# Forget gate and index key in one product, the meta tokens' square sums moved, and the spatial bias added by VectorE

## The reference

```
h = rms_norm(x, norm_g)
(a_u, a_v, a_z, b_q, b_c, b_qi, b_ki, b_wi, b_z, c_b, c_c, c_x, c_z,
 d_q, d_k, d_v, d_f, d_z, gates) = split(h @ w_in)

# branch a: spatial gating
v = layer_norm(a_v, ln_g, ln_b)                       # in chunks of 128 tokens, 4 groups of 128
mixed = einsum('gts,bcsge->bctge', tril(w_s), v) + b_s[token, group]
y_a = a_u * mixed * silu(a_z)

# branch b: a sparse attention; k_idx = b_ki (64 columns) picks each query's keys
score = sum_h b_wi[h] * relu(b_qi[h] . b_ki)          # the best 64 keys of each query are kept

# branch d: forgetting attention; d_f has 4 columns, one for each head
cum = cumsum(log_sigmoid(d_f + b_f))
logits = q . k / sqrt(128) + cum[query] - cum[key]

# second layer, ahead of its first product
hn = rms_norm(concat([meta_tokens, x']), norm1_g)
```

## Time and profile before

| | |
|---|---|
| median of three runs | 1201.8 us |
| span of the profiled execution | 1201.2 us |
| its time beyond the median | -0.6 us |
| PE busy | 1056.9 us (88%) |
| DVE busy | 491.7 us (41%) |
| ACT busy | 356.6 us (30%) |
| POOL busy | 387.8 us (32%) |
| chain that ended last, by engine | PE 60%, DMA 27%, DVE 8% |

### The profile page before, as it was taken

One profiled execution on the slowest core, in us unless ns is written; L12 is line 12 of the kernel. 1 busy time (PEld: TensorE's weight loads), 2 busy tenths in 40 slices (PEclk: granted clock), 3 DMA queues, 4 the chain that ended last, 5 costly groups with the idle time before them and its releaser, 6 DMA issues.

```text
span 1201.2 us, 20207 instructions
## 1 busy us (share of the span) xinstructions
PE 1056.9 (88%) x8237; PEld 852.8 (71%) x8237; DVE 491.7 (41%) x973; ACT 356.6 (30%) x536; POOL 387.8 (32%) x176
## 2 busy tenths in 40 slices
PE   9999999999999999999999998977676676767776
PEld 7999999999999999798989787443333333333334
DVE  4447944701125886667854413221111111111113
ACT  4544253444447557234252103100000000000002
POOL 4867568887877766133030000000000000000000
PEclk8999899999999998999999999998888888888898
DMA  6645446466656444113221685999999999999994
GB/s 232 197 127 157 121 143 201 148 185 185 191 167 205 154 143 140 53 54 140 80 91 43 276 332 213 417 428 428 428 428 428 428 428 429 428 428 428 428 413 178
DMA packets 41552, 303.95 MB, mean 253 GB/s; under 512 B 4869, under 2 KB 5253, under 8 KB 27786
## 3 DMA queue, kind: packets, MB, share of 16 engines
q1 hardware_dynamic: 41194, 302.43, 66.4%
q10 hardware_dynamic: 288, 0.52, 0.1%
HBM read 301.89 MB, written 1.05 MB: 252 GB/s over the span
## 4 chain that ended last, share of the span: by engine, by line
PE 60%; DMA 27%; DVE 8%; issue 1%; ACT 1%; SPq 1%; POOL 1%; DVEq 0%; ACTq 0%; POOLq 0%
DMA arena<-down 20%; PE bank L447 11%; PE bank L448 11%; PE bank L449 11%; PE bank L818 9%; PE bank L1273 4%; DMA weights<-gate_up 4%; PE bank L1256 3%; DMA arena<-gate_up 3%; PE bank L782 1%; DVE arena L1948 1%; PE bank L1227 1%; PE bank L1285 1%; PE bank L1018 1%; PE bank L997 1%
## 5 line engine op out<-in xcount | busy, mean ns | idle before, releaser
L2733 POOL TENSOR_TENSOR rounded<-weights,rounded 128x1024 fp32r<-128x1024 f32 x152 | 368.6, 2452 | 175.7 <-ACT rounded L1350 164.0
L447 PE MATMUL bank<-rounded 128*128 128x256 f32 (+2 forms) x784 | 223.0, 284 | 0.7 <-POOL rounded L2733 0.7
L449 PE MATMUL bank<-rounded 128*128 128x256 f32 (+2 forms) x784 | 221.7, 283 | 0.0
L448 PE MATMUL bank<-rounded 128*128 128x256 f32 (+2 forms) x784 | 221.5, 282 | 0.0
L1350 ACT ACTIVATE rounded<-weights 128x1024 fp32r<-128x1024 f32 x146 | 147.1, 1052 | 85.0 <-PE bank L449 56.0
L447 PEld LDWEIGHTS bank<-rounded 128*128 128x128 f32 (+1 forms) x784 | 147.8, 189 | 2.9 <-POOL rounded L2733 1.2
L448 PEld LDWEIGHTS bank<-rounded 128*128 128x128 f32 (+1 forms) x784 | 147.1, 188 | 0.6 <-issue 0.5
L449 PEld LDWEIGHTS bank<-rounded 128*128 128x128 f32 (+1 forms) x784 | 146.7, 187 | 0.2
L447 PE MATMUL bank<-rounded,rounded 128*128 128x256 f32 (+3 forms) x456 | 131.8, 289 | 2.1 <-DVEq L2178 0.8
L448 PE MATMUL bank<-rounded,rounded 128*128 128x256 f32 (+3 forms) x456 | 130.4, 286 | 0.0
L449 PE MATMUL bank<-rounded,rounded 128*128 128x256 f32 (+3 forms) x456 | 130.2, 286 | 0.0
(11 more groups left out here) (444 smaller groups left out, 1348.5 us busy)
## 6 DMA issues: line engine op xcount, KB each, us to landing
weights<-front SPq DMA_DIRECT2D x152, 512.0 KB, 4.3
arena<-down SPq DMA_DIRECT2D x30, 2048.0 KB, 20.6
weights<-gate_up SPq DMA_DIRECT2D x28, 2048.0 KB, 33.4
arena<-gate_up SPq DMA_DIRECT2D x28, 2048.0 KB, 33.2
weights<-front SPq DMA_DIRECT2D x8, 2048.0 KB, 8.3
arena<-gate_up SPq DMA_DIRECT2D x4, 1536.0 KB, 32.9
weights<-gate_up SPq DMA_DIRECT2D x4, 1024.0 KB, 15.3
arena<-down SPq DMA_DIRECT2D x4, 1024.0 KB, 8.0
```

The source lines that it names most:

```text
L447: nc.tensor.matmul(out, a[0], b[1], start=start, stop=False)
L448: nc.tensor.matmul(out, a[0], b[0], start=False, stop=False)
L449: return nc.tensor.matmul(out, a[1], b[0], start=False, stop=stop)
L2733: nc.gpsimd.tensor_tensor(lo, raw[q % RAW], hi.bitcast(f32), ALU.subtract).then_inc(sem("w_lo"), 1)
```

## The change

1. The columns of the weight block are laid out anew, with the index key's 64 ahead of the forget gate's 4, and both are one product of 68 columns. The forget values then lie on partitions 64 to 67 (the slice `F`), and so do `sel` and `b_f`.
2. The square sums of the meta tokens leave the start and get a fill of their own, `meta_rows` in bank 4, behind the first group. What DVE and ACT make of them is moved behind the scaled `c` and the index key.
3. `b_s` is loaded to all 128 partitions, the eight matmuls that added it (one row of ones by `b_s`) are gone, and DVE adds it to the two banks in place ahead of the products of branch a.

```diff
@@ tensor engine
             f = begin("rms_rows", (2,))
-            pe.wait_ge(sem("squares"), 5)
-            for k in range(KD):
-                nc.tensor.matmul(f.bank[:, SEQ:SEQ + META], ones, meta_sq[:, k, :], start=k == 0, stop=k == KD - 1)
             pe.wait_ge(sem("rstd"), 1)
             token_rows(f, rstd1)
             warm_up(banks[5], 2)
...
-            ff_, fk, fc = begin("f", WK, 0), begin("ki", PJ, 0), begin("c", WK, 0)
-            last = {}
+            fk = begin("ki", PJ, 0)
+            turn[WK] += 1
+            fc = begin("c", WK, 0)
...
                 matmul3(fc.bank[:, 0:P + 4], rows_of(k, 0, P), part(w, at, P + 4), first, stop)
-                last["f"] = matmul3(ff_.bank[0:NH, 0:SEQ], part(w, at + 132, NH), rows_of(k), first, stop)
-                last["ki"] = matmul3(fk.bank[0:IDX, 0:SEQ], part(w, at + 136, IDX), rows_of(k), first, stop)
-            end(ff_, last["f"])
-            end(fk, last["ki"])
+                last = matmul3(fk.bank[0:IDX + NH, 0:SEQ], part(w, at + 132, IDX + NH), rows_of(k), first, stop)
+            end(fk, last)
...
             end(fc, last)
+            f = begin("meta_rows", (4,))
+            pe.wait_ge(sem("squares"), 5)
+            for k in range(KD):
+                last = nc.tensor.matmul(f.bank[:, 0:META], ones, meta_sq[:, k, :], start=k == 0, stop=k == KD - 1)
+            end(f, last)
...
-                        nc.tensor.matmul(o, av[:, t, gr * P:(gr + 1) * P], wsT[:, gr, :], start=True, stop=False)
-                        last = nc.tensor.matmul(o, ones[0:1, :], bs[0:1, gr * P:(gr + 1) * P], start=False, stop=True)
+                        last = nc.tensor.matmul(o, av[:, t, gr * P:(gr + 1) * P], wsT[:, gr, :], start=True, stop=True)
@@ scalar engine
-            act.wait_ge(sem("variance"), 2)
-            nc.scalar.activation(meta_var, meta_var, ACT.Sqrt).then_inc(sem("deviation"), 1)
             quarter_hi(5)
...
-            f = got("f")
+            f = got("ki")
...
+            act.wait_ge(sem("variance"), 2)
+            nc.scalar.activation(css, css, ACT.Sqrt).then_inc(sem("deviation"), 1)
             act.wait_ge(sem("variance"), 3)
-            nc.scalar.activation(css, css, ACT.Sqrt).then_inc(sem("deviation"), 1)
+            nc.scalar.activation(meta_var, meta_var, ACT.Sqrt).then_inc(sem("deviation"), 1)
@@ vector engine, behind the copy of the index key
+            meta_bank = got("meta_rows")
+            link(nc.vector.tensor_scalar(meta_var, meta_bank.bank[:, 0:META], 1.0 / D, EPS, ALU.mult, ALU.add))
+            dve.sem_inc(sem("variance"), 1)
...
+            dve.wait_ge(sem("deviation"), 3)
+            meta_row = meta_bank.bank[:, META:2 * META]
+            link(nc.vector.reciprocal(meta_row, meta_var))
+            for k in range(KD):
+                last = nc.vector.scalar_tensor_tensor(meta_n[:, k, :], res[:, k, 0:META], col("norm1_g", k), meta_row,
+                                                      ALU.mult, ALU.mult)
@@ vector engine, behind top_scores(1)
+            for i in range(2):
+                f = got(f"mx{i}")
+                mixed = f.bank[:, :].rearrange("p (j t s) -> p j t s", j=2, t=TT)
+                b_s = bs[:, 2 * i * P:(2 * i + 2) * P].rearrange("p (j s) -> p j s", j=2).unsqueeze(2).to_broadcast([P, 2, TT, P])
+                link(nc.vector.tensor_tensor(mixed, mixed, b_s, ALU.add))
             for i in range(2):
                 times(f"mx{i}", i, y[0][:, 2 * i:2 * i + 2, :], "az", "y0", cpad[:, 2 * i:2 * i + 2, 0:SEQ])
```

More of the change, by code:

```diff
@@ L421, in build @@
         FRONT = A["front"]
+        F = slice(IDX, IDX + NH)
         def two(bank):
@@ L606, in _ @@
                 for j in range(2):
-                    last = nc.tensor.matmul(f.bank[:, j * SEQ:(j + 1) * SEQ], sel[0:NH, 2 * i + j, 0:P], ff[0:NH, 4, :],
+                    last = nc.tensor.matmul(f.bank[:, j * SEQ:(j + 1) * SEQ], sel[F, 2 * i + j, 0:P], ff[F, 4, :],
                                             start=True, stop=True)
@@ L1412, in _ @@
             last.then_inc(sem("css"), 1)
-            f = got("f")
+            f = got("ki")
             act.wait_ge(sem("cols_in"), 16)
-            link(nc.scalar.activation(ff[0:NH, 0, :], f.bank[0:NH, 0:SEQ], ACT.Identity, bias=col("b_f")[0:NH]))
-            act.sem_inc(free[f.b], 1)
+            link(nc.scalar.activation(ff[F, 0, :], f.bank[F, 0:SEQ], ACT.Identity, bias=col("b_f")[F]))
+            act.sem_inc(sem("css"), 1)
+            act.wait_ge(sem("variance"), 2)
+            nc.scalar.activation(css, css, ACT.Sqrt).then_inc(sem("deviation"), 1)
             act.wait_ge(sem("variance"), 3)
-            nc.scalar.activation(css, css, ACT.Sqrt).then_inc(sem("deviation"), 1)
+            nc.scalar.activation(meta_var, meta_var, ACT.Sqrt).then_inc(sem("deviation"), 1)
             evacuate("qi", qi, "qiki")
-            link(nc.scalar.activation(ff[0:NH, 1, :], ff[0:NH, 0, :], ACT.Abs))
-            link(nc.scalar.activation(ff[0:NH, 1, :], ff[0:NH, 1, :], ACT.Exp, scale=-1.0))
-            nc.scalar.activation(ff[0:NH, 1, :], ff[0:NH, 1, :], ACT.Ln, bias=1.0).then_inc(sem("ln_f"), 1)
+            link(nc.scalar.activation(ff[F, 1, :], ff[F, 0, :], ACT.Abs))
+            link(nc.scalar.activation(ff[F, 1, :], ff[F, 1, :], ACT.Exp, scale=-1.0))
+            nc.scalar.activation(ff[F, 1, :], ff[F, 1, :], ACT.Ln, bias=1.0).then_inc(sem("ln_f"), 1)
             evacuate("dq0", dq[:, 0:2, :], "dq", scale=P ** -0.5)
@@ L1888, in _ @@
             dve.sem_inc(free[sums.b], 1)
-            nc.vector.tensor_scalar(meta_var, row_bank.bank[:, SEQ:SEQ + META], 1.0 / D, EPS, ALU.mult,
-                                    ALU.add).then_inc(sem("variance"), 1)
+            dve.sem_inc(free[row_bank.b], 1)
             link(nc.vector.tensor_tensor(both_g, cols[:, COLS["final_g"][0]:COLS["final_g"][1]],
                                          cols[:, COLS["norm1_g"][0]:COLS["norm1_g"][1]], ALU.mult))
-            dve.wait_ge(sem("deviation"), 2)
-            meta_row = row_bank.bank[:, SEQ + META:SEQ + 2 * META]
-            link(nc.vector.reciprocal(meta_row, meta_var))
-            for k in range(KD):
-                last = nc.vector.scalar_tensor_tensor(meta_n[:, k, :], res[:, k, 0:META], col("norm1_g", k), meta_row,
-                                                      ALU.mult, ALU.mult)
-            link(last)
-            dve.sem_inc(free[row_bank.b], 1)
             f = got("c")
@@ L1908, in _ @@
                                         NH ** -0.5 * IDX ** -0.5, None, ALU.mult)
-            dve.wait_ge(sem("deviation"), 3)
+            dve.wait_ge(sem("deviation"), 2)
             link(nc.vector.reciprocal(css, css))
@@ L1921, in _ @@
                     nc.vector.tensor_copy(two_rows_r[a:a + 4, 4 * half:4 * half + 4], ident[a:a + 4, a:a + 4])
+            dve.wait_ge(sem("deviation"), 3)
[4 more added lines that the diff above has]
+                                                      ALU.mult, ALU.mult)
+            link(last)
+            dve.sem_inc(free[meta_bank.b], 1)
             evacuate("bq0", bq[:, 0:2, :], "bq")
@@ L1929, in _ @@
             dve.wait_ge(sem("ln_f"), 1)
-            link(nc.vector.scalar_tensor_tensor(ff[0:NH, 2, :], ff[0:NH, 0, :], 0.0, ff[0:NH, 1, :], ALU.min, ALU.subtract))
-            link(nc.vector.memset(ff[0:NH, 1, :], 1.0))
-            nc.vector.tensor_tensor_scan(ff[0:NH, 3, :], ff[0:NH, 1, :], ff[0:NH, 2, :], 0.0, ALU.mult, ALU.add).then_inc(sem("forget"), 1)
+            link(nc.vector.scalar_tensor_tensor(ff[F, 2, :], ff[F, 0, :], 0.0, ff[F, 1, :], ALU.min, ALU.subtract))
+            link(nc.vector.memset(ff[F, 1, :], 1.0))
+            nc.vector.tensor_tensor_scan(ff[F, 3, :], ff[F, 1, :], ff[F, 2, :], 0.0, ALU.mult, ALU.add).then_inc(sem("forget"), 1)
             dve.wait_ge(sem("forget"), 1)
-            nc.vector.tensor_scalar(ff[0:NH, 4, :], ff[0:NH, 3, :], -1.0, None, ALU.mult).then_inc(sem("forget"), 1)
+            nc.vector.tensor_scalar(ff[F, 4, :], ff[F, 3, :], -1.0, None, ALU.mult).then_inc(sem("forget"), 1)
             f = got("cT")
@@ L2960, in lay_out @@
     chunks = lambda a: a.reshape(-1, P).T
-    b_f = np.concatenate([I["fox_b_f"][0], np.zeros(P - NH, I["fox_b_f"].dtype)])[:, None]
+    b_f = np.zeros((P, 1), I["fox_b_f"].dtype)
+    b_f[IDX:IDX + NH, 0] = I["fox_b_f"][0]
     cols = [chunks(a) for a in (I["norm_g"], I["final_g"], I["conv_w"], I["dsa_kv_g"])] + [b_f]
```

11 lines of the change are left out of this document (6 added, 5 removed).

## The result

The changed kernel takes 1207.5 us, the median of four runs (1206.82 to 1209.39), beside 1201.7 us before in the same comparison (four runs, 1199.1 to 1202.69). The ratio is 1.0052, with a 95% interval of 1.0034 to 1.0071: slower by some 6 us. Forecast were 1204.2 us with a range of 1199.6 to 1207.4, so the time lies 0.1 us above the range.

The account below looks back on a forecast made before the run. PE was taken to bound the kernel to 101 us, DVE alone from 101.0 to 153.2, then PE again. Terms -2.3 + 3.5 + 1.2 = +2.4 us on a 1201.8 median gave 1204.2 us, range 1199.6 to 1207.4.

Parts of the forecast that it names:

- Part 1: Start, without the square sums: L516 at about 10.9, 2.0 us earlier; first product -1.9; clock back from about 16.9.
- Part 2: First group: one product of 68 columns saves 2.8 us over 8 k; group ends at 21.0, -4.1 in all.
- Part 3: Square sums behind the first group, ahead of `qi`: 16 passes cost 1.8 us, ends 1.6 and 3.1.
- sum up to 101 us: -2.3: Start in total, PE and DVE: -4.1 + 1.8; ends -3.4 (clock rises earlier) and -1.0 (sums cost 3.1).
- Part 4: PE's mix without the bias matmuls: 1.8 us instead of 8.2; PE gains 7.8 but nothing at L592, held by DVE.
- Parts 5 and 6: DVE ahead of `fo1`'s release: bias additions 1.8 us, meeting with an earlier POOL 1.7, together +3.5 us.
- Part 7: PE stands some 11 us at `bl1` and `bl2`, then runs at half clock: +1.2 us, ends 0 and 3.
- The base: Kernel before: profiled span 1201.2 us, median of the runs 1201.8; the 0.6 between them is kept.
- Rival A: Whole kernel: PE is the bound throughout, -10.1 us, 1191.7 us; chance 6%.
- Rival B: Not slower: meeting POOL costs DVE no more than the earlier 3.1 us, clock soon back; -0.1, 1201.7 us; 24%.
- Rival C: Clock low one stretch longer after PE's wait, or L2024 misses POOL's gap, or both: 1206.3 us; 24%.
- Rival D: Start fails: sums cost 3.1, 68-column product is slower, or `bq1` waits for POOL: 1205.6 us; 8%.

Follow-up runs that it names:

- the one with the additions doubled: The changed kernel with each of DVE's two spatial-bias additions made twice; only profiled, span 1206.8 us, `fo1` released at 157.15.
- the first faster order: Kernel before plus 68 columns and VectorE bias, square sums at the start; `fo` releases and branch b's `softmax_in` ahead of additions and branch a: 0.9932, 1194.5 us.
- the kernel with the twelve warm-up products: The changed kernel with 12 warm-up matmuls of 512 columns in PE's long wait, ahead of branch b's logits: 1.0029 of before.
- the faster order: VectorE releases `fo0`, `fo1` and does branch b's `softmax_in` before additions and branch a: 0.9932 with square sums at the start, 0.9934 in the changed kernel.
- the spread version: The changed kernel with the eight square-sum matmuls spread one by one among the second products of the first group: 1.0042 of before.
- the single product: The changed kernel with only one of the eight square-sum products (two passes instead of sixteen): 1.0019 of before.

## Why the prediction missed

**Part 1** was right in its start (L518 at 10.77, forecast 10.9). That the clock would be back at 16.9 held in some executions only: it was about 13.6 in this profile and 17.1 in the one with the additions doubled. That the first group gained 5.0 us and not 4.1 is thus mostly luck. (The 21.0 of the prediction is the end of its products for the first 128 tokens, here 20.2; the other tokens follow to 22.6.) **Part 2** was right: -2.8 forecast, -3.0 measured alone.

**The step that failed is Part 3, and with it the "sum up to 101 us: -2.3"** with its ends of -3.4 and -1.0. The profile shows -0.2. It priced the sums behind the group as 1.8 us of busy time and put what they do to the clock at nothing. In times of all runs the step shows in the parts made alone: the product -3.0 (forecast -2.8), the bias +5.2 (+4.7), the moved sums +2.0 [+0.8, +3.2] (+0.5), the largest miss of the three. The sums' own time was nearly right, 1.90 us at full clock. In the execution with the additions doubled the clock did not fall behind them:

```profile
23.91 1.90 PE L554 MATMUL bank<-arena 128*128 128x16 f32 x16
```

There ScalarE empties `qi` at 31.70, 1.9 us before the 33.61 of the kernel before, which is close to the forecast. But that execution then has the clock at half from 85.4 to 88.8:

```profile
82.17 1.99 PE L610 MATMUL bank<-arena 4*128 4x256 f32 x8
84.63 4.57 PE L595 MATMUL bank<-arena 128*128 128x128 f32 x16 [0.47 <-DVEq L1998]
```

and the lead at 101 us is 0.3.

Part of the miss needs no fall at all. Two profiles have the clock at 2.4 GHz up to `qi` and differ until there only in the place of the sums and of what is made of them: the first faster order (at the start) and the kernel with the twelve warm-up products (behind the group).

```profile
11.47 0.69 PE L518 MATMUL bank<-arena 128*128 128x128 f32 x4
22.76 0.33 PE L449 MATMUL bank<-rounded 128*128 128x256 f32 x1
```

```profile
10.76 0.71 PE L518 MATMUL bank<-arena 128*128 128x128 f32 x4 [0.92 <-DVE arena L1865]
23.82 0.37 PE L449 MATMUL bank<-rounded 128*128 128x256 f32 x1
```

Leaving the start wins 0.7 us there, because PE waits 0.9 us for `rstd` anyway, and `qi` starts 1.1 us later. In the pair with 6.8 us of low clock at the start (without the move, and with the additions doubled) it starts 0.7 us later (24.93 and 25.66). The forecast took the 2.0 us of Part 1 from sums that ran at half clock in the earlier trace rows, and then priced the same sums at full clock.

I had not asked what the sums do to the clock either. Nor had I seen that a lead won at the start can be taken back at the next thin place (a stretch with little work for PE), the eight 4-row passes near 84 us (L607 before, in full clock throughout), which my rows did not include. The low clock before 101 us, added up over windows of one microsecond, is 6.8 us before; in nine kernels with the sums, or one of them, behind the group it is 3.4 to 10.2, 10.2 in four of them, and each of the nine has a fall at 22 to 32 or near 84 us; in the other four with the sums at the start it is 0 to 6.8, with no such fall. These are profiles of one execution each. What the timings settle is less: the move alone costs 0.17% [0.07, 0.27], the change with and without it differs by 0.27% with overlapping intervals, and the faster order by 0.02%, with overlapping intervals too. That every profile with the sums moved has such a fall, and none with them at the start, is shown; how much of the 6 us they are in the median run stays open, and so does why the fall comes at 24 us in one execution and at 85 in another. That narrow passes in a row cause it was not borne out by the spread version, and the single product left a fall at 84.

**Part 4** was right: the mix takes 1.95 us (forecast 1.8), PE gains 7.8, the dip at 133 is gone, and none of it reaches the end.

**Parts 5 and 6** were right in sum (3.5 forecast, 3.2 in the profile) and wrong in their shares. I put 1.8 on the additions and 1.7 on the meeting with POOL. It is 0.6 and 2.6, because the additions fill time in which POOL would have held VectorE. The Trainium skill (SBUF — State Buffer, Who interferes with whom) says that a VectorE instruction with at most one SBUF input, outside the two-port modes, is free of GpSimd. The additions at 0.69 beside a busy POOL agree, and I should have drawn the other half: here such instructions cost less than their own time (0.6 of 1.5 us), as they stand where the others would be held.

**Part 7** was right in kind and too small in size: 1.9 us measured, 1.2 forecast (ends 0 and 3). The twelve warm-up products took it away.

**The base** was some 1.7 us too high in span for the median, as the first section tells, 1.2 of it between 475 and 515 us, so a shift read in the traces came out smaller than one between medians.

Rival A fell: PE's 7.8 us did not reach the end, though with `fo` released first and the softmax ahead of branch a the time comes near to what A gave (1191.7 forecast for a PE-bound kernel, 1194.5 reached). Rival B fell by the release at 156.1. Rival C's total (1206.3) is the nearest to 1207.5, but by luck: its longer cold clock came at 24 us, not at 150, where the cost was 1.9. Its other condition, L2024 missing POOL's gap, did come (L2029 took 1.98), in a total of 3.2 and not the 4.8 it was priced at. Rival D, the start not doing what it says, names the right place, for another reason than those it gave.

## What to carry to other kernels

Before work is taken from an engine that waits, find the release it waits for and move that release forward in the other engine's order: here a new order on VectorE turned a loss of 0.5% into a gain of 0.7%. An engine made faster off the path still wakes others earlier (ScalarE, then POOL), and they meet the bound engine at another place. Work that stands where an engine waits costs less there than its busy time, and its whole time where it is moved into a dense stretch: compare the place it leaves with the place it goes to, at the same clock. Time won ahead of a thin stretch of PE is only won if the granted clock stays up behind it, so the clock belongs in the sum wherever small passes are moved.

## What the runs showed of the hardware

The clock at the start differs between executions of the same instructions. PE's instructions up to the end of the first group are the same in the kernel with only the 68 columns and in the one that adds the bias on VectorE to it. In the first the clock never left 2.4 GHz before 22 us; in the second it was at half from 11.1 to 18.0. The first faster order has the same start as the second on every engine, and its clock never left 2.4 GHz there either. The sixteen passes in the kernel with only the 68 columns, where they took 3.1 us in the earlier trace rows:

```profile
9.72 1.94 PE L530 MATMUL bank<-arena 128*128 128x16 f32 x16
```

The Trainium skill (TensorE: Matmul & The Clock Gate, What's actually happening) says that how many matmuls run cold varies from run to run of one kernel; these profiles agree for the start, and show that it also holds for falls in the middle of a busy PE. A granted clock that is read in one profile is thus a draw. My 16.9 us was one; the range had an end for an earlier rise, but none for a fall behind the sums.
